# A hybrid attention backbone on one core: value products in two runs of three, four buffers of transposed probabilities, other columns for the context sums

## What is computed

```
logits = [einsum(q_rot, k_latent), einsum(q_raw, k_cached)] * scale      # latent queries
p = softmax(concatenate(logits, axis=-1))                                # + a sink in the windowed group
out = p[..., :512] @ v_latent + p[..., 512:] @ v_cached
# context queries: softmax(q_ctx @ k_ctx.T * scale) @ v_ctx
mod = silu(cond) @ w_ada + b_ada                                         # 1024 x 6144 per layer, "conditioning"
```

## Time and profile before

| | us |
|---|---|
| median of 3 runs | 1806.75 (1806.15 to 1808.81) |
| the profiled execution | 1807.65 |
| its span, first to last instruction | 1805.9 |
| attention, layer 0 | about 178 to 394 of the span |
| attention, layer 1 | about 1055 to 1262 |

### The profile page before, as it was taken

The page is one execution under the profiler, slowest core; times in us unless marked ns, Lnnn a source line. Parts: engine busy times, 40 slices in busy tenths (PEclk is TensorE's granted clock), DMA queues, the critical chain, the costliest instruction groups (busy, mean ns, idle before and its releaser), DMA issues.

```text
span 1805.9 us, 30070 instructions
## 1 busy us (share of the span) xinstructions
PE 1712.2 (95%) x11625; PEld 1537.8 (85%) x11625; DVE 1114.8 (62%) x2279; ACT 626.3 (35%) x1257; POOL 150.2 (8%) x152
## 2 busy tenths in 40 slices
PE   5899999899999999999989989979999999999997
PEld 3899555469999999999989965545999999999997
DVE  3656666565766566566782856656576565665675
ACT  2421453453432222322242235436243322222223
POOL 0351010120000000000004402011100000000000
PEclk7899999999999999999999999999999999999998
DMA  8331442332222222222312322212223222222211
GB/s 273 110 103 36 143 146 94 117 120 68 71 82 70 80 71 70 81 70 80 89 47 67 95 78 94 94 48 87 89 70 94 71 70 74 77 70 81 70 59 59
DMA packets 188438, 156.53 MB, mean 87 GB/s; under 512 B 7824, under 2 KB 175284, under 8 KB 188340
## 3 DMA queue, kind: packets, MB, share of 16 engines
q1 hardware_dynamic: 188340, 155.19, 28.1%
HBM read 151.86 MB, written 3.31 MB: 86 GB/s over the span
## 4 chain that ended last, share of the span: by engine, by line
PE 85%; DVE 6%; DMA 3%; ACT 3%; issue 2%; POOL 1%; SPq 0%; DVEq 0%; ACTq 0%
PE PS L1106 81%; PE PS L1110 4%; DMA RW<-in_w_ada_dram 2%; DMA RW<-in_w_in_dram 1%; DVE H_lo L1627 1%; POOL SS L762 1%; DVE H_lo L1876 1%; DVE QTR L1566 1%; DVE X L1676 0%; ACT PT L781 0%; DVE ST L1827 0%; ACT H_hi L781 0%; POOL W_lo L740 0%; DVE XN_b L1614 0%; DVE KTR L1566 0%
## 5 line engine op out<-in xcount | busy, mean ns | idle before, releaser
L1106 PE MATMUL PS<-H_hi,W_lo 128*128 128x384 f32 (+1 forms) x1728 | 416.7, 310 | 0.0
L1106 PE MATMUL PS<-H_hi,W_hi 128*128 128x384 f32 (+1 forms) x1728 | 416.5, 310 | 0.0
L1106 PE MATMUL PS<-H_lo,W_hi 128*128 128x384 f32 (+1 forms) x1728 | 416.4, 310 | 0.0
L1106 PEld LDWEIGHTS PS<-H_lo,W_hi 128*128 128x128 f32 x1728 | 275.7, 189 | 0.0
L1106 PEld LDWEIGHTS PS<-H_hi,W_lo 128*128 128x128 f32 x1728 | 275.6, 189 | 0.0
L1106 PEld LDWEIGHTS PS<-H_hi,W_hi 128*128 128x128 f32 x1728 | 274.7, 189 | 0.8 <-issue 0.8
L781 ACT ACTIVATE W_hi<-RW 128x1024 fp32r<-128x1024 f32 (+1 forms) x176 | 183.9, 1050 | 190.1 <-PE PS L1106 161.7
L1945 DVE TENSOR_SCALAR CF<-U,VT 128x644 f32<-128x644 f32 x88 | 49.0, 556 | 268.7 <-ACT U L781 268.4
L1106 PE MATMUL PS<-G_hi,W_hi 128*128 128x384 f32 (+1 forms) x704 | 171.7, 310 | 0.0
L1106 PE MATMUL PS<-G_lo,W_hi 128*128 128x384 f32 (+1 forms) x704 | 171.4, 310 | 0.0
L1106 PE MATMUL PS<-G_hi,W_lo 128*128 128x384 f32 (+1 forms) x704 | 170.6, 308 | 0.0
(11 more groups left out here) (170 smaller groups left out, 2438.2 us busy)
## 6 DMA issues: line engine op xcount, KB each, us to landing
RW<-in_w_ada_dram SPq DMA_DIRECT2D x96, 512.0 KB, 4.4
RW<-in_w_up_dram SPq DMA_DIRECT2D x88, 512.0 KB, 3.8
RW<-in_w_down_dram SPq DMA_DIRECT2D x44, 512.0 KB, 3.6
RW<-in_w_in_dram SPq DMA_DIRECT2D x28, 512.0 KB, 3.9
RW<-in_w_out_dram SPq DMA_DIRECT2D x16, 512.0 KB, 3.4
RW<-in_w_in_dram SPq DMA_DIRECT2D x8, 352.0 KB, 3.2
out_dram<-OUT SPq DMA_DIRECT2D x5, 512.0 KB, 3.1
XIN<-in_x_sample_dram SPq DMA_DIRECT2D x4, 512.0 KB, 6.5
```

The costliest lines, as they stand in the source:

```text
L1106: return nc.tensor.matmul(out, lhsT, rhs, start=start, stop=stop, skip_group_check=True)
```

## The change

Head 2 of layer 0 now reads: Q Q V2 V3 V4 ADA P5 Y S0 P0 S1 P1 S2 P2 V5 V0 V1 ADA S3 P3 Y S4 P4, and K K behind P4 where new keys are due. The first V2 V3 V4 and Y are of head 0, the rest of head 1. In detail:

- V of k = TT, 0, 1 stand together behind S2 and P2, with the head's second chunk behind them and before S3; V of k = 2, 3, 4 stand together behind the next head's Q, with its first chunk behind them.
- The copies of the sums have a step of their own, `("Y", h, k)`. The context sum is copied behind P3, the latent sum behind the next head's first P. The context sum of an even head goes to columns 256 to 383 of bank 6 on partitions 0 to 63, that of an odd head to columns 0 to 127 on partitions 64 to 127, which the latent sums don't use. PE waits for the context sum's `y_lo` before k = 2, and for the latent sum's before the next head's k = TT.
- `PT` has four buffers, two of them in `PT_more`, which lies over a weight slot that is not in use then.
- DVE no longer divides the fifth tile at once, but at the next S or at the first P of its head. ACT does a waiting exponential behind a copy of P or a step Q, too.

```
+RUN = 2
     late = []
+    def last_values(v):
+        return v[RUN + 1:]
+    def at_once(h, t, v):
+        return t[:4] + v[:RUN + 1] + t[4:] + [("Y", h, TT)] + last_values(v) + [("Y", h, QT)]
     for h in range(HEADS):
         t, v = probs(h - 1) if h else ([], [])
         if h == 8:
-            order += t[:1] + late + t[1:2]
-            for x in range(2, len(t)):
-                order += v[x - 2:x - 1] + t[x:x + 1]
-            order += v[-2:]
+            order += late + [("Y", h - 2, QT)] + at_once(h - 1, t, v)
             t, v, late = [], [], []
...
-        order += late + [("T", ("Q", h, 0)), ("T", ("Q", h, 1))]
+        order += [("T", ("Q", h, 0)), ("T", ("Q", h, 1))]
         if h == 3:
             order.append(("PREP", 1))
-        order += [("ADA", todo[0])] + t[:1]
+        order += late + todo[:1] + t[:1]
+        if late:
+            order.append(("Y", h - 2, QT))
         for q in range(NQ):
             order.append(("S", h, q))
-            order += t[q + 1:q + 2] + v[q:q + 1]
+            order += t[q + 1:q + 2]
+            if q == 2:
+                order += v[:RUN + 1] + todo[1:]
+            if q == 3 and t:
+                order.append(("Y", h - 1, TT))
             if h == 7:
                 order += mla[3 * q:3 * q + 3]
-            if q == 3 and len(todo) > 1:
-                order.append(("ADA", todo[1]))
-        late = v[5:]
+        late = last_values(v)
...
     t, v = probs(HEADS - 1)
-    order += late + t[:1] + [("MOVE",)] + t[1:2]
-    for x in range(2, len(t)):
-        order += v[x - 2:x - 1] + t[x:x + 1]
-        if x == 3:
-            order.append(("SEL",))
-    order += v[-2:]
+    order += late + t[:1] + [("Y", HEADS - 2, QT), ("MOVE",)] + t[1:4] + v[:RUN + 1] + [("SEL",)] + t[4:]
+    order += [("Y", HEADS - 1, TT)] + last_values(v) + [("Y", HEADS - 1, QT)]
...
+        def turned(i):
+            return PT[:, i % 4, :] if i % 4 < 2 else PT_more[:, i % 4 - 2, :]
         def y_parts(k, r0):
             if k == TT:
-                return [(r0, 0, CTX0, CTX0 + P)]
+                return [(r0, QHALF - 4 * r0, CTX0, CTX0 + P)]
...
-                if i >= 2:
-                    values_done(eng, l, i - 2)
+                if i >= 4:
+                    values_done(eng, l, i - 4)
...
-                    elif e[0] == "V" and e[2] in (TT, QT):
+                    elif e[0] == "Y":
...
-                        values_done(act, l, i)
+                        values_done(act, l, i if k == QT else i + RUN)
...
-                    if waiting and (e[0] == "V" or e[0] == "MOVE"):
+                    if waiting and (e[0] in ("V", "MOVE") or e[0] == "T" and e[1][0] in ("P", "Q")):
                         exponentials(*waiting)
...
-                        if k in (TT, 0) and yi:
-                            pe.wait_ge(y_lo, l * (3 * HEADS) + yi)
+                        if k == TT and h:
+                            pe.wait_ge(y_lo, l * (3 * HEADS) + 3 * h)
+                        elif k == RUN:
+                            pe.wait_ge(y_lo, l * (3 * HEADS) + 3 * h + 1)
...
-                        if e[2] == QT:
-                            normalise_probs(*waiting)
-                            waiting = None
```

More of the change, by code:

```diff
@@ L188, in attention_order @@
     late = []
+    def last_values(v):
+        return v[RUN + 1:]
+    def at_once(h, t, v):
+        return t[:4] + v[:RUN + 1] + t[4:] + [("Y", h, TT)] + last_values(v) + [("Y", h, QT)]
     for h in range(HEADS):
         t, v = probs(h - 1) if h else ([], [])
+        todo = [("ADA", chunks.pop(0)) for _ in range(
+            1 + (len(chunks) > HEADS - h if h % 3 == 0 else len(chunks) >= 2 * (HEADS - h)))]
         if h == 8:
-            order += t[:1] + late + t[1:2]
-            for x in range(2, len(t)):
-                order += v[x - 2:x - 1] + t[x:x + 1]
-            order += v[-2:]
+            order += late + [("Y", h - 2, QT)] + at_once(h - 1, t, v)
             t, v, late = [], [], []
@@ L198, in attention_order @@
             order += [("T", ("K", kv_of(h), 0)), ("T", ("K", kv_of(h), 1))]
-        order += late + [("T", ("Q", h, 0)), ("T", ("Q", h, 1))]
+        order += [("T", ("Q", h, 0)), ("T", ("Q", h, 1))]
         if h == 3:
             order.append(("PREP", 1))
-        todo = [chunks.pop(0) for _ in range(1 + (len(chunks) > HEADS - h if h % 3 == 0 else len(chunks) >= 2 * (HEADS - h)))]
-        order += [("ADA", todo[0])] + t[:1]
+        order += late + todo[:1] + t[:1]
+        if late:
+            order.append(("Y", h - 2, QT))
         for q in range(NQ):
             order.append(("S", h, q))
-            order += t[q + 1:q + 2] + v[q:q + 1]
+            order += t[q + 1:q + 2]
[3 more added lines that the diff above has]
+                order.append(("Y", h - 1, TT))
             if h == 7:
                 order += mla[3 * q:3 * q + 3]
-            if q == 3 and len(todo) > 1:
-                order.append(("ADA", todo[1]))
-        late = v[5:]
+        late = last_values(v)
         if h == 7:
@@ L287, in backbone_program @@
         TBP = sb("TBP", [P, 2, 4 * HD])
-        sb("W_lo_1_to_3", [P, 3 * RMAX])
+        PT_more = sb("PT_more", [P, 2, NLAT])
+        sb("W_lo_2_to_3", [P, 2 * RMAX])
         K = sb("K", [P, K_N])
@@ L485, in evac_fill @@
                 i = 6 * h + P_SEQ.index(k)
-                if i >= 2:
-                    values_done(eng, l, i - 2)
+                if i >= 4:
+                    values_done(eng, l, i - 4)
                 c0, c1 = (0, P) if k == TT else (P * queries(h, k)[0], P * queries(h, k)[1])
-                copy(PT[:, i % 2, c0:c1], bank[:, c0:c1]).then_inc(done, 1)
+                copy(turned(i)[:, c0:c1], bank[:, c0:c1]).then_inc(done, 1)
             elif kind == "Q":
@@ L1362, in _ @@
                         pe.wait_ge(tr_ev[m_ % 2], l * NEV[m_ % 2] + (m_ // 2 + 1))
-                        yi = 3 * h + (k != TT)
-                        if k in (TT, 0) and yi:
-                            pe.wait_ge(y_lo, l * (3 * HEADS) + yi)
+                        if k == TT and h:
+                            pe.wait_ge(y_lo, l * (3 * HEADS) + 3 * h)
+                        elif k == RUN:
+                            pe.wait_ge(y_lo, l * (3 * HEADS) + 3 * h + 1)
                         kv = kv_of(h) - 4 if h >= 8 else kv_of(h) % 2
@@ L1371, in _ @@
                         for x, a0, a1 in value_parts(h, k):
-                            mm(PS[HD * x:HD * (x + 1), 6, a0:a1], v_ap(h // 4, kv, tile), PT[:, i % 2, a0:a1],
-                               k in (TT, 0), k in (TT, QT)).then_inc(pv_mm[x], 1)
+                            b0 = y_parts(k, HD * x)[0][1] if k == TT else a0
+                            mm(PS[HD * x:HD * (x + 1), 6, b0:b0 + a1 - a0], v_ap(h // 4, kv, tile),
+                               turned(i)[:, a0:a1], k in (TT, 0), k in (TT, QT)).then_inc(pv_mm[x], 1)
                     elif e[0] == "ADA":
```

## The result

The changed kernel takes 1835.4 us (median of 4 runs, 1832.87 to 1836.05) against 1807.53 for the kernel before on the same chip (4 runs): a ratio of 1.0152, 95% interval 1.0134 to 1.0169. It is 1.5% slower: 27.9 us by the medians, 25.2 by the two profiled executions (1832.87 and 1807.65). The forecast was 1826 with a range of 1810 to 1845.

The account below looks back on a forecast made before the run. It took the tensor engine (PE), 95% busy, as the bound; per layer 5 x 1.1 + 1.2 + 1.0 + 0.3 + 1.6 - 4 x 0.1 = 9.2, twice 18.4, on 1807.65 gave 1826 us, range 1810 to 1845.

Parts of the forecast that it names:

- The stalls: End of a head: the second query transpose waits for ACT's copy of P4, a PE stall of 1.4 us.
- S2's wait for exponential 0: First half of a head: S2 starts at +3.67 where PE was free at +3.02; such a head gains 0.1 us.
- What PE saves: Value products grouped in threes: 0.34 us per product behind another, 1.4 per head, 33 over 24 heads if PE never waits.
- five heads with key transposes: Per layer, heads with key transposes before the query transposes: waits on ACT's and DVE's copies make each 1.1 us longer.
- the other heads (2, 4 and 6): Heads without key transposes: end-of-head stall eats the saving, first half gains 0.1 us each, counted for four per layer.
- (a): Head 0: second chunk moves ahead of S3 while loads are scarce, and a chain to head 1 is exposed: +1.2 us per layer.
- (b): Behind head 7: context-sum copies and DVE's subtractions delay the next steps, fewer switches give part back: +1.0 us per layer.
- (c): Head 8, with no value products beside it: only the later last scaling costs, +0.3 us per layer.
- (d): The last head: ACT's steps in order take longer than the same work before, and V2 of head 10 waits: +1.6 us per layer.
- Rival 3: The forecast's stalls plus a falling clock, 1.5 us more in each of ten key-transpose heads: 1841 us, chance 0.18.
- The costs set at nothing: Further buffers make no copy longer; chunk loads keep their number and come no closer together than before: no cost.
- Rivals 1 and 2: First: PE's saving holds, stalls hidden, 1775 to 1791, chance 0.10. Second: saving and stalls cancel, 1804 to 1810, chance 0.06.

Follow-up runs that it names:

- tails_divided: keys_queries_early plus, behind heads 7 and 11, the context sum copied right behind its run and the fifth tile divided at once: 1781.3 us, ratio 0.9845.
- filled_gaps: The changed kernel with extra PE products put in its pauses, in layer 1 only (outputs wrong, times alone count): 1826.2 us, ratio 1.0095.
- before_keys_queries_early: The kernel before, value products still one by one, with the next head's key and query transposes moved earlier: 1809.1 us, ratio 0.9995.
- run_before_q: The changed kernel with the run V2, V3, V4 put ahead of the next head's key and query transposes: 1829.4 us, ratio 1.0115.
- storage_alone: The kernel before with only the change's storage (four PT buffers, other columns for context sums), old order of steps: 1811.05 us, ratio 1.0004.
- keys_queries_early: y_early with the next head's key and query transposes moved earlier and the second run behind the next head's chunk: 1790.7 us, ratio 0.9899.
- y_early: The changed kernel with the context sum copied right behind the run that ends it, ahead of the second chunk: 1813.4 us, ratio 1.0021.

## Why the prediction was right, step by step

**The stalls, the forecast's mechanism: right, and close in time.** Counted from S3 of head 2 (220.97), forecast against measured: exponential and its sum over +3.31, +3.31 (224.09 + 0.19); copy of P4 over +4.25, +4.24; second query transpose +4.30, +4.29; chunk +5.95, +5.99; next S0 +7.13, +7.16. In the head with key transposes the second key transpose comes at +4.01 (forecast 4.30), the first query transpose at +5.48 (5.70), S0 at +8.79 (8.95). The 0.2 to 0.3 between them are there from the first stop on: ACT's copy of P4 starts 3.37 behind S3 there (239.24), since its operations overlap more than in the head before. S2's wait for exponential 0 was forecast as 0.65 and the row shows 0.47.

**What PE saves: right.** The run of three takes 1.44, as forecast (0.10 + 1.35). The saving of 33 us shows where the waits are covered: PE is busy 34.0 us less in the stages of tails_divided than in the earlier trace rows, a part of which is fewer half-clock stretches. The Trainium skill ("TensorEngine Tiling (Array Packing)", Key Properties) says that a change of tiling mode drains the array; the 0.34 per value product put behind another agrees with it; no run here isolates the drain. The figure that followed from that rule alone, 1775, is 33 us below the kernel before; tails_divided is 29.7 below it (1781.3 against 1811.0), with help from steps that the change doesn't have, so the nearness is partly luck.

**The terms.** Differences of periods after and before, from the profiled executions:

| term, forecast | layer 0 | layer 1 |
|---|---|---|
| five heads with key transposes, 5 x 1.1 | 8.1 | 8.5 |
| of these, clock up: 1.1 each | 1.16 and 1.04 | 1.17 and 1.40 |
| the other heads (2, 4 and 6), -0.4 | -0.6 | -0.6 |
| (a) head 0, +1.2 | +0.3 | +0.7 |
| (b) head 7 to 8, +1.0 | -0.2 | +1.4 |
| (c) head 8, +0.3 | +0.8 | +0.5 |
| (d) the tail, +1.6 | +1.5 | +1.4 |

The 1.40 is head 9 of layer 1, with part of a half-clock stretch in it. The -0.2 of (b) is flattered: head 7 of layer 0 has two half-clock stretches before and one after, and without that it would be some +1.3 (an estimate at 1.5 for one), as in layer 1. Without the second row they add up to 9.9 and 12.0, and 1.2 more of layer 1 lies ahead of its first score product, where a half-clock stretch (1069.4) has moved to. The 1.1 for a head with key transposes was the right size where the clock held. The step that was mis-sized is to have left the clock out of that sum. Rival 3 came in part: the clock falls in five of the ten heads, in four of them newly, and these four lost 2.4, 2.5, 2.8 and 2.9. The ten heads lost 16.6 and not 11.0; these 5.6 are most of the 25.2 - 18.4 = 6.8 that the forecast was short by the profiled executions. filled_gaps shows the cause for layer 1; for layer 0 it is argued from the same pattern. Since the stretches vary between executions, the size of this term is that of one profile. Why head 8 lost 0.8 and 0.5 and not 0.3 was not followed.

**Two slips in the sum.** It subtracts 0.1 for four other heads per layer, and there are three (2, 4 and 6); this is 0.2 us. And the terms that it names for its own range (0.5 to 1.5 per head with key transposes, 2 to 6 for the irregular places) add up to 1816 to 1834 and not to 1815 to 1837. The median of 1835.4 lies just above them, the profiled 1832.87 inside; what is missing is again the clock.

**The remaining +2.2 outside attention** were forecast as nothing. A half-clock stretch at 468.7 in the MLP of layer 0, which the kernel before doesn't have, would be some 1.5 of it. filled_gaps has it too (467.7), so it doesn't come from layer 1. before_keys_queries_early, with the value products in the old order, has one as well (460.2), and run_before_q has none; what sets it off was not tried.

**(a) was mis-sized:** 1.2 forecast, 0.3 and 0.7 measured. The chain did come out into the open: the first P of head 1 now waits 1.16 for DVE's division in layer 0 and 1.30 in layer 1, where it waited for nothing before. But the wait for the chunk's DMA ahead of it fell from 1.98 to 0.93 and from 1.89 to 0.80, and the forecast had not taken that off.

**The costs set at nothing held:** the storage (storage_alone 1.0004), and the loads of chunks.

**Rivals 1 and 2** did not come, but the condition that rival 1 named, the copy of P4 landing before PE needs the bank, is what keys_queries_early brought about by another order, and the time came out at 1791, the figure given there for half of the 33 us. That the number is the same is a coincidence: the order is another, and it is a sum of other terms.

**Expectations behind the prediction that failed.** before_keys_queries_early was argued from the waits for key and query copies alone; they went, but the loads of the chunks, which came closer together, took as much. In run_before_q the steps came where expected, and only the total was 4 us below the range, with seven half-clock stretches in place of twelve.

## What to carry to other kernels

Work that looks like pure cost in PE's stream (a lone product between two switches) may be the cover of another engine's chain. Before grouping it, add up what lies between the producer's last use of a bank and the next demand for it, in the strict order in which the copying engine takes its steps: here the exponential stood ahead of the copy, and 2.9 us of PE's work faced 4.3 of ACT's. Then move together with the group whatever waits for these copies: the grouping cost 28 us alone, and with keys and queries transposed earlier the whole was 18 us faster than the kernel before. Look at loads too when steps move: the same move without the grouping gained nothing, because two chunks came closer together. And a pause can have a second price: the half clock behind it, where it came, cost about 1.5 us here. Since such stretches vary from one execution to the next, compare heads with the same clock before reading a difference of 1 or 2 us.

## What the hardware showed beside this

- The granted clock fell to half for 3.4 us behind some pauses of PE and not behind others that look alike in the windows: busy 2.08 of 4.00 before 359.50 with a fall, and 2.08 of 4.00 before 242.50 without. Extra products in the pauses removed three falls at once (layer 1, 219.4 to 214.9 us). With the same order of steps the kernel before had two half-clock stretches in the attention of layer 1 and storage_alone four.
- In filled_gaps, products that start a new sum in columns 256 to 511 of bank 7 seem to have disturbed unfinished sums in columns 0 to 255 of the same bank, on the same partitions. This was inferred from the outputs being off; the sums were not read, and it was not isolated.
- The same edit can move the total by more than its own stalls, either way: y_early took away some 10 us of stalls in the regular heads and 20 us of time, and run_before_q made heads longer and the total no longer. Both have fewer half-clock stretches in the stages, eight and seven in place of twelve.
